# Sum of squares from the feature-major input, first score operands staged a block earlier, gated transposes begun inside the last gate block

## The reference

```python
def rms_norm(x, g):
    y = x * lax.rsqrt(jnp.mean(x * x, axis=-1, keepdims=True) + EPS)
    return y * g

h = rms_norm(x, norm_gain)
qa, ka, va, ga, qb, kb, vb, gb, qi, ki, wi = jnp.split(h @ w_in, offsets, axis=-1)
out_a = chunked_relpos_attention(qa, ka, va, rel_bias)       # 8 heads of 128, relative-position bias
out_b = dsa_sparse_attention(qb, kb, vb, qi, ki, wi, slopes)  # indexer scores, top 64 keys per query, ALiBi
y = concatenate([out_a * silu(ga), out_b * silu(gb)])
x = x + y @ w_out
return rms_norm(x, final_gain)
```

## Time and profile before

| what | value |
|---|---|
| median of 3 runs | 536.39 us |
| the profiled execution, time | 536.13 us |
| the profiled execution, span of its trace | 534.1 us |
| TensorE (PE) matmuls, share of the span | 98% |
| VectorE (DVE) | 65% |
| ScalarE (ACT) | 49% |
| GpSimd (POOL) | 6% |
| mean granted TensorE clock | 0.996 of full speed |

### The profile page before, as it was taken

The page is one execution under the profiler, slowest core; times in us unless marked ns, Lnnn a source line. Parts: engine busy times, 40 slices in busy tenths (PEclk is TensorE's granted clock), DMA queues, the critical chain, the costliest instruction groups (busy, mean ns, idle before and its releaser), DMA issues.

```text
span 534.1 us, 8164 instructions
## 1 busy us (share of the span) xinstructions
PE 523.7 (98%) x2789; PEld 451.1 (84%) x2789; DVE 345.1 (65%) x506; ACT 262.5 (49%) x378; POOL 29.4 (6%) x46
## 2 busy tenths in 40 slices
PE   8999999999999999999999999999999999999994
PEld 6899998888888888888888888888888888888883
DVE  6856685765667657568665767657576667556454
ACT  6865545344444344355364636354545445434342
POOL 1004042250000000000000000000000000000000
PEclk9999999999999999999999999999999999999998
DMA  8997976657555655664655554445444575665614
GB/s 293 394 308 218 274 219 196 200 175 276 174 185 192 196 196 195 194 184 137 193 161 158 176 172 161 162 167 185 157 157 157 179 270 182 196 198 170 213 50 157
DMA packets 60662, 104.53 MB, mean 196 GB/s; under 512 B 3536, under 2 KB 45408, under 8 KB 60128
## 3 DMA queue, kind: packets, MB, share of 16 engines
q1 hardware_dynamic: 58944, 98.78, 56.6%
q0 software_dynamic: 1264, 5.00, 3.1%
q10 hardware_dynamic: 432, 0.47, 0.3%
HBM read 101.34 MB, written 2.11 MB: 194 GB/s over the span
## 4 chain that ended last, share of the span: by engine, by line
PE 91%; DMA 4%; DVE 2%; ACT 1%; issue 0%; SPq 0%; DVEq 0%; ACTq 0%
PE acc L428 26%; PE acc L393 15%; PE acc L395 15%; PE acc L394 15%; PE acc L426 12%; DMA w_raw<-w_blocks 4%; PE aux L609 1%; DVE w_lo L976 1%; PE aux L494 1%; PE acc L431 1%; PE aux L613 1%; PE aux L588 1%; PE aux L598 1%; ACT w_hi L709 1%; DVE acts L1020 0%; PE aux L668 0%
## 5 line engine op out<-in xcount | busy, mean ns | idle before, releaser
L976 DVE TENSOR_TENSOR w_lo<-w_raw,w_hi 128x1024 fp32r<-128x1024 f32 x172 | 213.4, 1242 | 161.3 <-ACT w_hi L709 160.4
L709 ACT ACTIVATE w_hi<-w_raw 128x1024 fp32r<-128x1024 f32 x172 | 182.0, 1059 | 232.5 <-PE acc L395 114.7
L428 PE MATMUL acc<-acts,w_hi 128*128 128x512 f32 (+1 forms) x640 | 215.5, 387 | 0.0
L426 PE MATMUL acc<-acts,w_lo 128*128 128x256 f32 (+1 forms) x600 | 165.4, 276 | 0.6 <-DVE w_lo L976 0.6
L393 PE MATMUL acc<-w_hi,acts 128*128 128x512 f32 x376 | 148.0, 394 | 0.4 <-DVE acts L1357 0.4
L395 PE MATMUL acc<-w_hi,acts 128*128 128x512 f32 x376 | 146.6, 390 | 0.0
L394 PE MATMUL acc<-w_lo,acts 128*128 128x512 f32 x376 | 146.3, 389 | 0.0
L428 PEld LDWEIGHTS acc<-acts,w_hi 128*128 128x128 f32 x640 | 119.0, 188 | 20.2
L426 PEld LDWEIGHTS acc<-acts,w_lo 128*128 128x128 f32 x600 | 113.3, 189 | 1.5 <-DVE w_lo L976 0.9
L395 PEld LDWEIGHTS acc<-w_hi,acts 128*128 128x128 f32 x376 | 70.6, 188 | 15.0
L393 PEld LDWEIGHTS acc<-w_hi,acts 128*128 128x128 f32 x376 | 70.6, 188 | 14.6 <-issue 0.6
(11 more groups left out here) (165 smaller groups left out, 354.7 us busy)
## 6 DMA issues: line engine op xcount, KB each, us to landing
w_raw<-w_blocks SPq DMA_DIRECT2D x140, 512.0 KB, 4.0
w_raw<-wo_blocks SPq DMA_DIRECT2D x32, 512.0 KB, 3.3
w_raw<-w_blocks SPq DMA_DIRECT2D x8, 256.0 KB, 5.5
v<-x SPq DMA_DIRECT2D x2, 1024.0 KB, 10.5
v<-x POOLq DMA_DIRECT2D x1, 2048.0 KB, 9.3
qk<-xT SPq DMA_DIRECT2D x7, 256.0 KB, 6.0
o<-ext_dram POOLq DMA_DIRECT2D x1, 1024.0 KB, 9.2
fgain<-final_gain POOLq DMA_DIRECT2D x1, 1024.0 KB, 8.2
```

What stands on the lines that cost most here:

```text
L426: nc.tensor.matmul(acc[:, bank:bank + n], w_lo4[:, u % RING, q, c], a_hi[:, k, tokens], start=False, stop=False)
L428: last = nc.tensor.matmul(whole, w_hi4[:, u % RING, q, c], acts[:, k, :, tokens], start=(k == 0), stop=(k == KT - 1))
L709: nc.scalar.activation(flat(w_hi[:, s, :, :]), w_raw[:, s, :], ACT.Copy).then_inc(hi_done, 1)
L976: nc.vector.tensor_tensor(flat(w_lo[:, s, :, :]), w_raw[:, s, :], flat(w_hi[:, s, :, :]).bitcast(f32), ALU.subtract).then_inc(lo_done, 1)
```

## The change

It has three parts.

1. The token-major load of `x` (two DMAs) and its two squares go. ScalarE squares `xT_land` in eight pieces of 128 x 512 into `x_square` (a view of `o`), VectorE adds these up (seven additions, 128 x 512, and one of 128 x 256) into `x_sum`, which holds for each partition and token the sum over the 16 feature tiles. TensorE sums over the partitions: once with a matrix of ones as stationary operand (256 columns, giving the sum for `rk` on all partitions) and twice with `x_sum` as stationary operand and one column of ones (giving `ssq` for the tokens on partitions). These stand between units 2 and 3 of block 1. The `rk_cols` products and copies go; `rk` and `rstd` are each made by a square root on ScalarE and a reciprocal on VectorE.
2. `stage_q(0, 1, 4)` and `stage_rest(0, 1, 0)` move from behind the value block 9 to ahead of it.
3. On TensorE unit 7 of block 17 is taken out of `gate_block`; `y_transposes(0)` stands ahead of it, 1 and 2 behind it, and each of 3 to 7 behind a unit of block 18. `y_hi(q)` waits for unit q of block 17 instead of the whole block.

```diff
--- before.py
+++ after.py
@@ SyncE @@
                 load_features(u, w_blocks[0, :, :, :].rearrange("u p c -> p u c"))
-                if 1 <= u < 1 + TM:
-                    sp.dma_start(x_nat[:, u - 1, :], x[:, u - 1, :]).then_inc(x_landed[u - 1], 16)
@@ TensorE @@
-            for u in range(4):
+            for u in range(3):
                 feature_unit(1, u, 1, CHUNK)
+            pe.wait_ge(cleared, 3 + HEADS)
+            pe.wait_ge(summed, UNITS)
+            nc.tensor.matmul(aux[2][:, 0:T], ones_mat[:, :], x_sum[:, 0:T], start=True, stop=True)
+            for m in range(TM):
+                last = nc.tensor.matmul(aux[3][:, m:m + 1], x_sum[:, m * P:m * P + P], ones[:, :], start=True, stop=True)
+            last.then_inc(ssq_made, 1)
+            feature_unit(1, 3, 1, CHUNK)
...
-            pe.wait_ge(cleared, 3 + HEADS)
-            pe.wait_ge(rk_cols_done, 2)
-            for m in range(TM):
-                nc.tensor.matmul(aux[2 + m][:, 0:P], ones_mat[:, :], rk_cols[:, m, :],
-                                 start=True, stop=True).then_inc(rk_made, 1)
...
                 value_pair(i + 4, used, used)
-                unit(g, 7)
 
             pe.wait_ge(feat_out, 19)
             gate_block(G_GATE, 0)
-            with pe.Fori(1, 4) as i:
+            unit(G_GATE, 7)
+            with pe.Fori(1, 3) as i:
                 g = i + G_GATE
                 pe.wait_ge(feat_out, 20)
                 both_out(i + 3)
                 gate_block(g, i)
-
+                unit(g, 7)
+            both_out(6)
+            gate_block(G_OUT - 1, 3)
...
-            for q in range(4):
-                y_transposes(q)
+            y_transposes(0)
+            unit(G_OUT - 1, 7)
+            y_transposes(1)
+            y_transposes(2)
             both_out(token_count(G_OUT - 2))
             for u in range(UNITS):
                 pe.wait_ge(ylo_done, u + 1)
                 unit(G_OUT, u)
-                if u < 4:
-                    y_transposes(u + 4)
+                if u + 3 < UNITS:
+                    y_transposes(u + 3)
@@ ScalarE @@
-            nc.scalar.preload_act_table(ACT.Sqrt)
+            def square_x(u):
+                nc.scalar.activation(x_square[:, u, :], flat(xT_land[:, UK * u:UK * u + UK, :]),
+                                     ACT.Square).then_inc(squared, 1)
+
+            square_x(0)
+            square_x(1)
             split_hi(0, 8)
+            square_x(2)
+            square_x(3)
             split_hi(0, 9)
+            square_x(4)
+            square_x(5)
+            square_x(6)
+            split_hi(0, 10)
+            square_x(7)
+            split_hi(0, 11)
             act.wait_ge(nw_landed, 16)
             nc.scalar.activation(flat(nw_hi[:, :, :]), nw_raw[:, :], ACT.Copy).then_inc(nhi_done, 1)
-            split_hi(0, 10)
-            for m in range(TM):
-                act.wait_ge(x_landed[m], 16)
-                if m > 0:
-                    act.wait_ge(ssq_done, m)
-                nc.scalar.activation(o_flat[:, 0:D], x_nat[:, m, :], ACT.Square,
-                                     accum_out=ssq[:, m:m + 1]).then_inc(ssq_done, 1)
-                if m == 0:
-                    split_hi(0, 11)
...
             with act.Fori(G_VB, G_VA) as g:
                 value_block(g, g - G_VB)
-            value_block(G_VA, 3)
...
             act.wait_ge(feat_out, 8)
             stage_q(0, 1, 4)
+            value_block(G_VA, 3)
...
             def y_hi(q):
                 act.wait_ge(ytr_done, q + 1)
+                act.wait_ge(mm_done, (G_OUT - 1) * UNITS + (q + 1))
...
-            act.wait_ge(mm_done, G_OUT * UNITS)
             y_hi(0)
@@ VectorE @@
+            def add_square(u):
+                dve.wait_ge(squared, u + 1)
+                if u > 1:
+                    dve.wait_ge(summed, u - 1)
+                nc.vector.tensor_tensor(x_sum, x_sum, x_square[:, u, :], ALU.add).then_inc(summed, 1)
...
-            value_block(G_VA, 3, 3)
...
             stage_rest(0, 1, 0)
+            value_block(G_VA, 3, 3)
```

More of the change, by code:

```diff
@@ L103, in hybrid_block @@
         neg_slope = sb("neg_slope", [P, HEADS])
-        rk_cols = sb("rk_cols", [P, TM, P])
         ones_mat = sb("ones_mat", [P, P])
@@ L165, in hybrid_block @@
         nlo_done = sem("nlo_done")
-        x_landed = [sem(f"x_landed{m}") for m in range(TM)]
-        ssq_done = sem("ssq_done")
-        var_done = sem("var_done")
+        squared = sem("squared")
+        summed = sem("summed")
+        ssq_made = sem("ssq_made")
         std_done = sem("std_done")
@@ L180, in hybrid_block @@
         keys_out = sem("keys_out")
-        rk_cols_done = sem("rk_cols_done")
         rk_made = sem("rk_made")
@@ L239, in hybrid_block @@
         o_flat = o[:, :, :, :].rearrange("p b m c -> p (b m c)")
+        x_square = o_flat.rearrange("p (u c) -> p u c", u=UNITS)
+        x_sum = x_square[:, 0, :]
         bias_back = o_flat[:, D:2 * D].rearrange("p (h k) -> p h k", h=HEADS)
@@ L371, in _ @@
             pool.wait_ge(ext_stored, 16)
-            pool.wait_ge(ssq_done, TM)
+            pool.wait_ge(summed, UNITS)
             windows = bass.AP(tensor=ext_dram.tensor, offset=ext_dram.offset + 1,
@@ L751, in _ @@
                 split_hi(0, u)
-            nc.scalar.preload_act_table(ACT.Sqrt)
+            def square_x(u):
[3 more added lines that the diff above has]
+            square_x(1)
             split_hi(0, 8)
+            square_x(2)
+            square_x(3)
             split_hi(0, 9)
+            square_x(4)
[4 more added lines that the diff above has]
+            split_hi(0, 11)
             act.wait_ge(nw_landed, 16)
             nc.scalar.activation(flat(nw_hi[:, :, :]), nw_raw[:, :], ACT.Copy).then_inc(nhi_done, 1)
-            split_hi(0, 10)
-            for m in range(TM):
-                act.wait_ge(x_landed[m], 16)
-                if m > 0:
-                    act.wait_ge(ssq_done, m)
-                nc.scalar.activation(o_flat[:, 0:D], x_nat[:, m, :], ACT.Square,
-                                     accum_out=ssq[:, m:m + 1]).then_inc(ssq_done, 1)
-                if m == 0:
-                    split_hi(0, 11)
-            act.wait_ge(var_done, 1)
+            split_hi(0, 12)
+            nc.scalar.preload_act_table(ACT.Sqrt)
+            act.wait_ge(aux_read[2], 1)
+            nc.scalar.activation(rk[:, :], rk[:, :], ACT.Sqrt).then_inc(std_done, 1)
+            act.wait_ge(aux_read[3], 1)
             nc.scalar.activation(rstd[:, :], ssq[:, :], ACT.Sqrt).then_inc(std_done, 1)
-            split_hi(0, 12)
+            split_hi(0, 13)
             nc.scalar.preload_act_table(ACT.Exp)
-            split_hi(0, 13)
             act.wait_ge(rstd_done, 2)
@@ L786, in _ @@
             split_hi(0, 19)
-            for m in range(TM):
-                act.wait_ge(rk_made, m + 1)
-                nc.scalar.activation(rk[:, m * P:m * P + P], aux[2 + m][:, 0:P], ACT.Copy).then_inc(aux_read[2 + m], 1)
             features_low(1, 1, 1, QT)
@@ L1048, in _ @@
                                            ALU.max).then_inc(pen_step, 1)
+            def add_square(u):
[3 more added lines that the diff above has]
+                nc.vector.tensor_tensor(x_sum, x_sum, x_square[:, u, :], ALU.add).then_inc(summed, 1)
             split_lo(0, 8)
+            for u in range(1, 4):
+                add_square(u)
             split_lo(0, 9)
+            add_square(4)
+            add_square(5)
+            split_lo(0, 10)
+            add_square(6)
+            split_lo(0, 11)
+            add_square(7)
+            dve.wait_ge(summed, UNITS - 1)
+            nc.vector.tensor_tensor(x_sum[:, 0:T], x_sum[:, 0:T], x_sum[:, T:2 * T], ALU.add).then_inc(summed, 1)
             dve.wait_ge(nhi_done, 1)
@@ L1054, in _ @@
                                     ALU.subtract).then_inc(nlo_done, 1)
[L1055 to L1059, removed]
+            split_lo(0, 12)
+            dve.wait_ge(ssq_made, 1)
+            nc.vector.tensor_scalar(rk[:, :], aux[2][:, 0:T], 1.0 / D, EPS, ALU.mult, ALU.add).then_inc(aux_read[2], 1)
+            nc.vector.tensor_scalar(ssq[:, :], aux[3][:, 0:TM], 1.0 / D, EPS, ALU.mult,
+                                    ALU.add).then_inc(aux_read[3], 1)
+            dve.wait_ge(std_done, 2)
             nc.vector.reciprocal(rstd[:, :], rstd[:, :]).then_inc(rstd_done, 1)
+            nc.vector.reciprocal(rk[:, :], rk[:, :]).then_inc(rk_made, 1)
             dve.wait_ge(rstd_done, 1)
@@ L1065, in _ @@
                                            ALU.mult).then_inc(rated, 1)
-            for m in range(TM):
-                nc.vector.tensor_scalar(rk_cols[:, m, :], ident[:, :], rstd[:, m:m + 1], None,
-                                        ALU.mult).then_inc(rk_cols_done, 1)
             dve.wait_ge(rated, 2)
@@ L1072, in _ @@
                 nc.vector.tensor_copy(idx_rate0[rows[h], :], idx_rate[CHUNK:P, 0:1]).then_inc(rated, 1)
-            for c in (12, 13):
-                split_lo(0, c)
```

(4 more changed lines are left out.)

## The result

The changed kernel takes 533.67 us (533.43 to 534.02, 5 runs) against 536.39 (535.84 to 537.01, 5 runs) of the kernel before; the ratio is 0.9947, 95% interval 0.9934 to 0.9960. Timed again it was 533.85 us, ratio 0.9956 (0.9943 to 0.9968). Forecast were 534.2 us and a range from 533.6 to 535.2. The direction was right and so were the places where the time is won, but the size was too small: 2.0 us by the sum, 2.4 to 2.8 by the two ratios, and 0.9947 of 536.39 is 533.55, just outside the range. The second ratio gives 534.0, inside it, so that the range is missed at all is within the noise. That one term of the sum was too small does not hang on this: five traces show it further down.

The account below looks back on a forecast made before the run. TensorE was taken to bound the kernel, busy 523.7 of 534.1 us. Terms -0.54 - 0.92 - 0.58 = -2.04 us gave 534.1 from the profiled execution and 534.35 from the median; predicted 534.2, range 533.6 to 535.2.

Parts of the forecast that it names:

- Three stops, each removed: TensorE waits at 36 us, 241 us (first scores) and 437 us (output projection), losing 0.89, 0.92 and 0.58 us, would go.
- the first stop: TensorE's wait at 36 us, between units 2 and 3 of block 1, for a `w_lo` behind a DMA: 0.89 us.
- the signs named ahead: No PE wait at L424, L584, L391; unit 3 of block 1 at about 36.5; L516 gone; first scores 0.35 us.
- Part 2, -0.92: Staging moved before block 9 ends TensorE's stop at the first scores, 241 us: -0.92 us.
- Part 3, -0.58: Moved transposes let unit 0 of block 18 follow transposes 1 and 2 at once: -0.58 us.
- The next waits: At the output projection `y_lo(1)`, for unit 1, is late next, with 1.1 us left; `y_lo(2)` is covered by 1.2.
- Part 1, -0.54: Sum of squares: stop at 36 us gone -0.89, new products +0.80, L516 gone -0.45; bounds -0.74 and -0.14 us.
- 0.89 us lost: Stop at 36 us: from one L428 to the next 1.17 us with it, 0.28 without.
- L516: Work on TensorE at 54 us that part 1 removes, 0.45 us.
- 1.8 us of cover: In block 1 the sum is there at 33.9 us, TensorE comes to its wait at 35.66.
- The rival "slower": VectorE's chained additions end 5.4 us later, at 39.3; TensorE stops 3.6 us at its new wait: 537.8 us; chance 0.04.
- Products with one column: Four new TensorE instructions in block 1, bound by loading the stationary operand: 0.09 us apart, 0.36 to 0.76, taken as 0.36.

Follow-up runs that it names:

- the identity's kernel: Changed kernel without the two one-column products, VectorE taking `ssq` from the sums multiplied by the identity: 533.27 us, ratio 0.9947 against the kernel before.

## Why the prediction was right and wrong

**Three stops, each removed: right.** No wait of PE is left at L424, L584 or L391, and the body between the marks is 1.98 us shorter than in the trace of before, forecast 2.04. This agreement is no test of the price of the first stop, because that price was read from the same trace of before. Of the signs named ahead one did not come: unit 3 of block 1 starts at 35.91, not at 36.5, as TensorE arrives 0.54 us earlier than in that trace.

**Part 2, -0.92: right.** 0.92 in the trace, 1.0 us (0.5 to 1.5) alone.

**Part 3, -0.58: right.** 0.64 us (0.2 to 1.1) alone. The next waits were where I had put them: `y_lo(1)` ends at 436.83 and unit 1 starts at 437.81, a cover of 0.98 against 1.1 forecast.

**Part 1, -0.54: the term that failed, "0.89 us lost".** I read the price of the stop from one trace, and took it as a constant. It is the difference of two times, and both vary: TensorE's arrival (35.02 to 35.46 at the last L428) and the moment the split weights are there (36.43 to 37.00). Over the five traces with x loads it is 0.89, 1.20, 1.80, 1.77 and 1.41, mean 1.41, and removing it alone gave 1.56 us (0.9 to 2.2). The new products cost 0.88 instead of 0.80, as I had left out the slower first pair behind them. With -1.41 + 0.88 - 0.45 part 1 is -0.98, alone it measured -1.0 (0.5 to 1.4). L516 was right, 0.45. The corrected sum is -0.98 - 0.92 - 0.58 = -2.48 us, between the 2.4 and 2.8 of the two timings. The timings of the single parts would just admit the forecast's values too; what carries the correction is that each of the four later traces has a larger stop than the one I read. That I had the smallest of five was bad luck; to rest the term on one trace was the mistake. The range failed with the term: I put 0.4 us of scatter around a median where the removed stop itself varied by 0.9 us.

**"1.8 us of cover" for the sum: wrong, without harm.** It is about 0.5. The price of an addition was right, 0.76 with its wait (2.28 for three), and the eight and the splits among them run without a gap from 24.76 to 34.64. But I had the sum at 33.9, 0.7 too early, and the product of ones at 35.66, 0.5 too late: ScalarE still waits 1.0 us, until 23.66, for the first unit's weights in the changed kernel, so that the sums start late, and TensorE comes to the product at 35.12. The rival "slower", a stop at the new wait, was nearer than its 0.04: two more additions bring such a stop, and with the x loads in flight it is there.

**"Products with one column": right.** They are 0.09 apart, where one load by itself is recorded at 0.19, so the loads overlap with products. The Trainium skill (TensorE: Matmul & The Clock Gate, LDWEIGHTS) gives columns / 1.2 ns for a load, an estimate of 0.107 us each. The trace has 0.09 and so does not agree. All four cost 0.44 us with their restart, by the identity's kernel.

## What to carry to other kernels

A stop in a trace is the difference between two arrivals, and where one of them waits for a DMA and the other depends on the start-up, a single trace can price it badly (here 0.89 us, where five have 1.41 in the mean): take several, or remove the cause alone, before forecasting what its removal brings. Work that replaces a wait must be counted as work: here 0.88 us of small products ate most of what the stop had cost, and half of that was in four instructions of one column each, which 0.85 us of idle VectorE could replace; that version has the lowest median of this study, 533.27 us. And before a chain is moved in front of the busiest engine, find how long a delay it stands, with a dose of extra work: here it was about 0.5 us.

## What the runs showed of the hardware

By the distance of starts: the granted clock of TensorE fell to 0.50 behind a stop of 2.3 us in the middle of dense work and was 0.50 over the stretch from 38 to 44 us, and the execution took 539.74 us where those with the full clock took 536.3. With stops of 0.75 to 1.80 us all seven traces show 1.00 around the stop. But some executions of such kernels took longer at a lower mean granted clock without being traced: 3 of 12 with four more additions (537.3 us, 0.992 or 0.993), 1 of 11 with parts 2 and 3 (537.11, 0.993) and 1 of 24 of the kernel before, timed in the same set (538.94, 0.994). A stop can thus cost more than its own length.

A reciprocal on VectorE of 128 x 256 took 1.73 us, where an addition of that size takes 0.42 and a reciprocal of 128 x 2 takes 0.17. I had left it unpriced but bounded by 3 us, and it hid. Timeline of DVE of the changed kernel:

```profile
38.18 1.73 DVE L1086 RECIPROCAL rk<-rk 128x256 f32<-128x256 f32 x1
```
